# Seventy-eight TensorE matmuls into an unread PSUM bank behind the last output transposes of a streaming encoder layer

## The chip, the cores and the metric

The kernel runs on one core of a Trainium2 chip. The metric is the device time of one execution in microseconds (us), the median over a few executions. The profile is that of one execution, taken by the hardware profiler.

## The reference

One layer of a hybrid encoder is computed for 1024 prompt frames (one new stream) and 32 sample frames (a running stream with caches):

```python
h = rms_norm(x, g_mix);  z = h @ w_in
rq, rk, rv, rg, dq, dk, dv, ga, gb = split(z)
branch_a = (rms_norm(retention(rope(rq), rope(rk), rv)) * silu(rg)) @ w_ret_br
branch_b = (rms_norm(diff_attention(dq, dk, dv), g_dnorm) * (1 - lam_init)) @ w_da_br
x = x + (sigmoid(ga) * branch_a + sigmoid(gb) * branch_b) @ w_out
u = rms_norm(x, g_ffn) @ w_up
x = x + (silu(cg) * cv) @ w_down            # cg, cv: causal depthwise conv of u
x = x + sigmoid(rms_norm(x, g_ple) @ w_ple_gate) * (ple @ w_ple)
```

It returns y for both streams, the new keys and values, the retention states and the last rows for the convolution. The width is 1024, the hidden width 2816, all data are float32.

## The kernel before

Activations lie feature-major in SBUF: 128 features on the partitions, 1056 token columns (1024 prompt and 32 sample) in the free dimension, cut into three thirds of 352 (`THIRD`). Every large product is made of three matmuls on reduced float32 (`F32R`) operands, high by high, high by low and low by high (`three`, lines 639 to 641); `w_hi` and `w_lo` are the two parts of the weights in eight slots, `a_hi` and `a_lo` those of the activations. GpSimd splits the weights, SyncE loads them, ScalarE and VectorE empty PSUM. All work is placed by hand: each engine has one written-out program, and semaphores order them.

The change stands at the end of TensorE's program. There the last stage runs over eight feature tiles m: the gate product (`gate_product`, 72 matmuls of 352 columns), then the small product of the per-layer input (`ple_product`, 18 of them), and `out_rows(m - 1)` (line 1129) in between: nine transposes against `ident`, line 1141, that turn 128 features back into token rows, into PSUM banks 6 and 7 and, for the 32 sample rows, another bank. For m = 7 the transposes wait for VectorE third by third (`y_done`, lines 1138 to 1140). ScalarE copies banks 6 and 7 out (line 1755) and sends the rows to `y_prompt` (line 1759); VectorE copies the 32 sample rows (line 2332) and SyncE sends them (line 525).

Then the block closes (line 109): each engine drains its queue and adds to a semaphore, GpSimd waits until all have, and releases them all. ScalarE comes to its own drain only when the last stores have landed, since its program ends with waits on `y_st` and `ul_st` (lines 1769 to 1771).

Tile m = 7 uses weight slot 5 (`PG_SLOTS[7 % 3]`) for its gate; that slot, `a_hi` and `a_lo` are not written again. Banks 0 to 2 hold the last accumulators, 0, 6 and 7 the last output rows; bank 4 was last read for m = 6.

Of the kernel before, what the change touches and what calls it, by code (L numbers as in the profile page):

```python
# [22 lines left out]
P = 128  # L23
# [84 lines left out]
def kernel_program(nc, t):  # L108
    with ExitStack() as ctx:
        def sb(name, shape, dt=F32):  # L110
            return ctx.enter_context(nc.sbuf_tensor(name, shape, dt))
# [8 lines left out]
        w_hi = sb("w_hi", [P, SLOTS, 8 * P], F32R)  # L120
        w_lo_at = -(-nc.sbuf_base // 32) * 32
        w_lo = sb("w_lo", [P, SLOTS, 8 * P], F32R)

        x_late = nc.alloc_sbuf_tensor_at("x_late", [P, 4, D], F32, offset=w_lo_at + 4 * 4 * 8 * P)
        a_hi = sb("a_hi", [P, KT * NT], F32R)
        a_lo_at = -(-nc.sbuf_base // 32) * 32
        a_lo = sb("a_lo", [P, KT * NT], F32R)
# [16 lines left out]
        ps = ctx.enter_context(nc.psum_tensor("ps", [P, 8, 512], F32))  # L144
# [141 lines left out]
        at = nrm_at + 256  # L286
# [349 lines left out]
        def _(pe):  # L636
# [492 lines left out]
            def out_rows(m):  # L1129

                for part, (i0, i1) in enumerate(((0, 4), (4, 8), (8, 9))):
                    if part < 2 and m:
                        pe.wait_ge(S["y_ev"], 3 * m - 2 + part)
                    for i in range(i0, i1):
                        r = rows(i)
                        if m < 7:
                            if i == 0:
                                pe.wait_ge(S["y_done"], m + 1)
                        elif i in (0, 2, 5):
                            pe.wait_ge(S["y_done"], m + 1 + (0, 2, 5).index(i))  # L1140
                        last = pe.transpose(ps[0:r, row_bank(m, part), (i % 4) * P:(i % 4 + 1) * P],
                                            x(m)[:, i * P:i * P + r], ident[:, :])
                    last.then_inc(S["y_tr"], 1)
# [98 lines left out]
            last_ple_product()  # L1242
            out_rows(7)


        @block.scalar
        def _(act):
# [1136 lines left out]
```

## Time and profile before

| | |
|---|---|
| device time, median of 3 runs | 2210.62 us (2210.6 to 2211.06) |
| span of the profiled execution, first to last instruction | 2209.2 us |
| median less that span | 1.4 us |
| TensorE (PE) busy in the span | 2201.9 us, 13110 matmuls |
| weight loads (PEld) | 2088.3 us, 13110 |
| VectorE (DVE), ScalarE (ACT), GpSimd (POOL) | 1089.5, 704.5, 666.3 us |

The span is the time of the profiled execution itself, from its first to its last instruction; the 1.4 us to the median lie around it. A matmul's row lasts longer than the spacing of the starts, since matmuls are pipelined: the cost of one in a row of them is read from the distance between starts. Registers, branches, semaphores and DMA issues don't count as busy; they carry a q behind the engine's name (PEldq is TensorE's queue).

### The profile page before, as it was taken

How to read it: one execution, taken by the hardware profiler on the slowest of the kernel's cores; microseconds unless marked ns; L12 is line 12 of the kernel's file. 1: busy time of each engine (PE TensorE's matmuls, PEld its weight loads, DVE VectorE, ACT ScalarE, POOL GpSimd, SP SyncE). 2: the span in 40 equal slices, each digit the busy share in tenths (PEclk: the TensorE clock that was granted, in tenths of full speed). 3: DMA queues.
4: the chain of work that ended last, by engine and by line, in shares of the span. 5: the costliest groups of instructions: out<-in, count | busy, mean ns of one | idle time of the engine just before them, and what ended most of it. 6: DMA issues, size and time to landing. Idle time of an engine off the chain costs nothing.

```text
span 2209.2 us, 34227 instructions
## 1 busy us (share of the span) xinstructions
PE 2201.9 (100%) x13110; PEld 2088.3 (95%) x13110; DVE 1089.5 (49%) x2076; ACT 704.5 (32%) x1654; POOL 666.3 (30%) x368
## 2 busy tenths in 40 slices
PE   9999999999999999999999999999999999999999
PEld 9999777789898898998999999999999999999999
DVE  6212444555646456364155568676666663313432
ACT  5201333335555555555221131101111113434311
POOL 5422220230310401303152353233332226576420
PEclk9999999999999999999999999999999999999999
DMA  8622222230220301304652322222122226656311
GB/s 266 205 83 73 72 81 82 73 107 25 64 83 30 115 29 31 114 27 159 228 181 62 107 80 68 68 68 77 60 75 67 72 73 201 182 167 202 94 49 50
DMA packets 312670, 218.19 MB, mean 99 GB/s; under 512 B 16332, under 2 KB 303679, under 8 KB 312544
## 3 DMA queue, kind: packets, MB, share of 16 engines
q1 hardware_dynamic: 219802, 117.33, 18.4%
q10 hardware_dynamic: 92742, 99.15, 13.4%
q8 instruction: 83, 1.36, 0.3%
q14 instruction: 43, 0.35, 0.1%
HBM read 160.15 MB, written 56.29 MB: 98 GB/s over the span
## 4 chain that ended last, share of the span: by engine, by line
PE 99%; DVE 0%; DMA 0%; issue 0%; ACT 0%; ACTq 0%; DVEq 0%
PE ps L639 28%; PE ps L641 28%; PE ps L640 28%; PE ps L931 3%; PE ps L904 3%; PE ps L779 1%; PE ps L780 1%; PE ps L922 1%; PE ps L850 1%; PE ps L855 1%; PE ps L1066 1%; PE ps L852 1%; PE ps L907 0%; PE ps L868 0%; PE ps L1082 0%; PE ps L834 0%
## 5 line engine op out<-in xcount | busy, mean ns | idle before, releaser
L639 PE MATMUL ps<-a_hi,w_hi 128*128 128x352 f32 x2920 | 946.8, 324 | 0.0
L641 PE MATMUL ps<-a_hi,w_lo 128*128 128x352 f32 x2920 | 936.9, 321 | 0.0
L640 PE MATMUL ps<-a_lo,w_hi 128*128 128x352 f32 x2920 | 936.3, 321 | 0.0
L537 POOL TENSOR_SCALAR w_hi<-w_raw 128x1024 fp32r<-128x1024 f32 x150 | 162.9, 1086 | 1404.4 <-PE ps L641 659.9
L639 PEld LDWEIGHTS ps<-a_hi,w_hi 128*128 128x128 f32 x2920 | 547.8, 188 | 3.4 <-issue 2.7
L640 PEld LDWEIGHTS ps<-a_lo,w_hi 128*128 128x128 f32 x2920 | 548.9, 188 | 0.4
L641 PEld LDWEIGHTS ps<-a_hi,w_lo 128*128 128x128 f32 x2920 | 548.4, 188 | 0.0
L539 POOL TENSOR_TENSOR w_lo<-w_raw,w_hi 128x1024 fp32r<-128x1024 f32 x150 | 363.8, 2425 | 12.5
L639 PE MATMUL ps<-w_hi,a_hi 128*128 128x384 f32 (+1 forms) x768 | 283.3, 369 | 0.0
L641 PE MATMUL ps<-w_hi,a_lo 128*128 128x384 f32 (+1 forms) x768 | 273.3, 356 | 0.0
L640 PE MATMUL ps<-w_lo,a_hi 128*128 128x384 f32 (+1 forms) x768 | 273.0, 355 | 0.0
L614 POOL TENSOR_TENSOR w_lo<-w_raw,w_hi 128x1024 fp32r<-128x1024 f32 (+1 forms) x64 | 141.4, 2240 | 74.2 <-ACT w_hi L1687 74.2
L641 PEld LDWEIGHTS ps<-w_hi,a_lo 128*128 128x128 f32 x768 | 144.2, 188 | 11.4
L640 PEld LDWEIGHTS ps<-w_lo,a_hi 128*128 128x128 f32 x768 | 144.9, 189 | 9.9
L639 PEld LDWEIGHTS ps<-w_hi,a_hi 128*128 128x128 f32 x768 | 144.5, 188 | 10.1
L1640 ACT ACT_TABLE_LOAD x21 | 26.9, 1283 | 253.0 <-issue 253.0
L2203 DVE TENSOR_TENSOR scr<-ps,scr 128x704 f32<-128x704 f32 x44 | 39.2, 891 | 132.0 <-PE ps L641 132.0
L2211 DVE COPY u_last<-scr 128x4 f32 (+1 forms) x44 | 88.3, 2006 | 5.7
L2249 DVE TENSOR_TENSOR full<-full,ps 128x352 f32 (+1 forms) x24 | 12.4, 520 | 155.9 <-PE ps L641 155.9
L1884 DVE TENSOR_TENSOR scr<-ps,full 128x128 f32<-128x128 f32 (+3 forms) x72 | 25.7, 356 | 117.0 <-ACT full L1354 115.8
L1354 ACT ACTIVATE full<-ps,u_last 128x256 f32<-128x256 f32 (+1 forms) x36 | 17.0, 472 | 204.3 <-PE ps L641 192.9
L1640 ACT ACTIVATE scr<-scr 128x1058 f32<-128x1058 f32 x22 | 24.0, 1090 | 182.2 <-DVE scr L2219 182.2
(230 smaller groups left out, 2522.5 us busy)
## 6 DMA issues: line engine op xcount, KB each, us to landing
w_raw<-w_in SPq DMA_DIRECT2D x64, 512.0 KB, 4.3
w_raw<-w_down SPq DMA_DIRECT2D x48, 512.0 KB, 3.7
w_raw<-w_up SPq DMA_DIRECT2D x44, 512.0 KB, 3.8
hid_d<-scr ACTq DMA_DIRECT2D x22, 512.0 KB, 2.6
w_raw<-w_down SPq DMA_DIRECT2D x24, 384.0 KB, 3.3
scr<-gates_d ACTq DMA_DIRECT2D x24, 352.0 KB, 6.2
gates_d<-full ACTq DMA_DIRECT2D x13, 528.0 KB, 2.6
xt_d<-full ACTq DMA_DIRECT2D x1, 4224.0 KB
```

The lines of the kernel that those rows point to most:

```text
L537: pool.tensor_scalar(hi, raw, 1.0, 0.0, ALU.mult, ALU.add).then_inc(S["w_hi_done"], 1)
L539: pool.tensor_tensor(lo, raw, hi.bitcast(F32), ALU.subtract).then_inc(S["w_split"], 1)
L614: pool.tensor_tensor(w_lo[:, slot, 0:words], w_raw[:, j % RAW, 0:words], w_hi[:, slot, 0:words].bitcast(F32), ALU.subtract).then_inc(S["w_ ...
L639: pe.matmul(out, lhs[0], rhs[0], start=start, stop=False)
L640: pe.matmul(out, lhs[0], rhs[1], start=False, stop=False)
L641: return pe.matmul(out, lhs[1], rhs[0], start=False, stop=stop)
L904: last = pe.matmul(ps[0:r, score_bank(m, i) + b // 512, 0:n], q_t[:, i % 2, m, 0:r], k_t[:, m, first + b:first + b + n], start=True, stop= ...
L931: last = pe.matmul(ps[0:r, 7, 0:DV], a_t[0:n, b, 0:r], v_tok[0:n, vt, :], start=b == 0, stop=b == every - 1)
L1640: act.activation(row(1, CW), row(1, CW), ACT.Silu).then_inc(S["silu_done"], 1)
L1884: dve.tensor_tensor(bb[:, :, 0, :], x4[:, :, 1, :], sn, ALU.mult).then_inc(prods, 1)
L2203: dve.tensor_tensor(u[:, GAP:GAP + 2 * THIRD].rearrange("p (c n) -> p c n", c=2), src[:, 0:2, :], inv[:, 0:2 * THIRD].rearrange("p (c n) - ...
L2211: dve.tensor_copy(u_last[:, bass.ds(j + half * FT, 1), :].rearrange("p a (s w) -> p (a s) w", w=GAP), ends).then_inc(S["u_last_done"], 1)
```

## The change

Behind `out_rows(7)`, the last work of TensorE's program, 78 matmuls are added. They wait for no semaphore and add to none. All write bank 4, and nothing reads that bank afterwards.

```diff
             last_ple_product()
             out_rows(7)
+
+            def resident(n, at=0, m=P, stationary=w_hi[:, 5, 0:P], moving=a_hi, bank=4, times=6):
+
+                for _ in range(times):
+                    pe.matmul(ps[0:m, bank, 0:n], stationary[:, 0:m], moving[:, at:at + n], start=True, stop=True)
+
+            resident(512)
+            resident(352)
+            resident(264)
+            resident(352, at=32)
+            resident(352, at=8)
+            resident(264, at=264)
+            resident(352, stationary=a_hi[:, 4096:4096 + P], moving=w_hi[:, 5, :])
+            resident(256)
+            resident(352, m=64)
+            for _ in range(4):
+                for lhs, rhs, bank in ((w_hi, a_hi, 4), (w_hi, a_lo, 4), (w_lo, a_hi, 4)):
+                    pe.matmul(ps[:, bank, 0:264], lhs[:, 5, 0:P], rhs[:, 0:264], start=True, stop=True)
+            resident(128)
+            resident(32)
```

The loops are Python's: the program holds 78 separate matmuls, each with its weight load. By moving width they are 6 of 512 columns, 30 of 352 (five calls: two with a shifted start, one with the operands' parts exchanged, one with 64 stationary columns), 24 of 264, 6 of 256, 6 of 128 and 6 of 32. No other engine's program is touched.

## Rows read from the trace of the kernel before

**Rows 1.** The page: the span and the engines' busy time
```profile
span 2209.2 us, 34227 instructions
PE 2201.9 (100%) x13110; PEld 2088.3 (95%) x13110; DVE 1089.5 (49%) x2076; ACT 704.5 (32%) x1654; POOL 666.3 (30%) x368
PE 99%; DVE 0%; DMA 0%; issue 0%; ACT 0%; ACTq 0%; DVEq 0%
q8 instruction: 83, 1.36, 0.3%
```
**Rows 2.** The timeline of the last 3 us: start, duration, engine, line, shapes
```profile
2205.24 0.66 PE L1141 MATMUL ps<-ident,full 128*128 128x128 f32 x4 [0.44 <-DVE full L2329]
2205.82 0.59 ACT L1755 COPY scr<-ps 128x512 f32<-128x512 f32 x1 [0.46 <-PE ps L1141]
2206.44 0.38 ACTq L1759 DMA_DIRECT2D y_prompt<-scr  x1
```
**Rows 3.** Line 109, the block's close: operation, count, duration in ns, start in us
```profile
L109 PEldq DRAIN  x1: 700/700/700, 2205.2 to 2205.2; - x1
L109 ACTq DRAIN  x1: 8/8/8, 2209.0 to 2209.0; - x1
L109 PEldq EVENT_SEMAPHORE  x1: 51/51/51, 2209.2 to 2209.2; - x1
```
**Rows 4.** Stretches at the end: busy time by engine, granted clock, DMA share, GB/s
```profile
2200.00:2205.00 5.00, 4.69 (x33) 4.18 (x31) 3.30 (x7) 2.40 (x5) 0.00 (x0) 1.00 0.22 65
2205.00:2209.20 4.20, 0.66 (x4) 0.38 (x4) 0.46 (x2) 0.95 (x2) 0.00 (x0) 1.00 0.64 180
2205.00:2210.00 5.00, 0.66 (x4) 0.38 (x4) 0.46 (x2) 0.95 (x2) 0.00 (x0) 0.93 0.54 151
```
**Rows 5.** Timeline of TensorE in the last gate product, 352 columns
```profile
2197.51 0.32 PE L639 MATMUL ps<-a_hi,w_hi 128*128 128x352 f32 x1
2197.66 0.32 PE L640 MATMUL ps<-a_lo,w_hi 128*128 128x352 f32 x1
2197.82 0.32 PE L641 MATMUL ps<-a_hi,w_lo 128*128 128x352 f32 x1
...
2198.47 0.32 PE L639 MATMUL ps<-a_hi,w_hi 128*128 128x352 f32 x1
```
**Rows 6.** Timeline of TensorE, 512 columns, 128 stationary columns
```profile
256.93 0.39 PE L641 MATMUL ps<-w_hi,a_lo 128*128 128x512 f32 x1
...
258.30 0.40 PE L641 MATMUL ps<-w_hi,a_lo 128*128 128x512 f32 x1
```
**Rows 7.** The same with 64 stationary columns
```profile
248.51 0.39 PE L779 MATMUL ps<-w_hi,pair 128*64 128x512 f32 x1
...
249.88 0.39 PE L779 MATMUL ps<-w_hi,pair 128*64 128x512 f32 x1
```
**Rows 8.** Timeline of TensorE, narrow matmuls in a row
```profile
1.07 3.58 PE L710 MATMUL ps<-ones 128*128 128x128 f32 x16 [1.07 <-DVE ones L1776]
5.87 1.06 PE L710 MATMUL ps<-ones 128*128 128x128 f32 x8
27.62 0.68 PE L683 MATMUL ps<-ident,x_late 32*128 32x32 f32 x8
```
**Rows 9.** Groups by shape: line, engine, shapes, count, busy us, mean ns
```profile
L710 PE MATMUL ps<-ones 128*128 128x128 f32 x46 | 7.3, 324 | 1.1 <-DVE ones L1776 1.1
L683 PE MATMUL ps<-ident,x_late 32*128 32x32 f32 x8 | 0.7, 224 | 0.0
L639 PEld LDWEIGHTS ps<-a_hi,w_hi 128*128 128x128 f32 x2920 | 547.8, 188 | 3.4 <-issue 2.7
L779 PEld LDWEIGHTS ps<-w_hi,pair 128*64 128x64 f32 x96 | 12.9, 135 | 4.7
```
**Rows 10.** The chain of waits, float32 of 256 columns: start, length in us, engine, line, count
```profile
883.07 1.73 PE ps L931 x8
```

## The prediction

> **What bounds the kernel now.** I read the page first. TensorE is busy in 2201.9 of 2209.2 us, and 99% of the chain that ended last is TensorE's [rows 1]. So whatever is added to TensorE ahead of its last output would cost its full length. The change stands behind that output, where the share says nothing: there the question is what ends last in the final 4 us.
>
> For that I read the timeline of the tail. TensorE's last four transposes start at 2205.24 us and their row ends at 2205.90; ScalarE copies them out from 2205.82 and issues the last store at 2206.44 [rows 2]. Then no engine computes. The reader is to see in the stretches that between 2205.0 and 2209.2 TensorE is busy for 0.66 us and the DMA engines for 64% [rows 4]: the tail is the landing of the last store. The rows of line 109 show how it ends: TensorE's queue is drained at 2205.2 + 0.70 = 2205.9, ScalarE's only at 2209.0, and the release reaches TensorE at 2209.2 [rows 3]. TensorE therefore lies idle for 3.1 us behind its last transpose, and any work that is shorter than this would be free there. From the last engine's drain to the end of the span it takes 0.2 us.
>
> **What the change adds.** Nothing is removed or moved, no wait and no semaphore is added, and no DMA. 78 matmuls, each with a weight load, stand behind the last transpose in TensorE's queue. What is queued behind them is TensorE's drain, and GpSimd waits for that drain before it releases the engines. The outputs are not behind them: ScalarE, VectorE and SyncE wait for the transposes' semaphores, which are given before.
>
> The cost is the spacing of starts, not the length of a row, since two rows overlap. At 352 columns six starts take 2198.47 - 2197.51 = 0.96 us, so 0.160 us for one [rows 5]. At 512 columns it is (258.30 - 256.93) / 6 = 0.228 us [rows 6]. That is 0.455 and 0.446 ns a column: the cost goes by the columns, with hardly a fixed part. For 264 and 256 columns, which the trace doesn't show with reduced operands, I take 0.455 ns a column from the nearer width: 0.120 and 0.116 us. With 64 stationary columns the spacing is (249.88 - 248.51) / 6 = 0.228 us at 512 columns [rows 7], the same as with 128, so the call with m=64 is priced as the others. The exchanged operands and the shifted starts I price like the plain ones: the kernel already runs either order (activations stationary in rows 6, weights in rows 5) at nearly the same price a column. The shifts themselves have no row; they can't be cheaper than a plain one, and I hold their risk with the upper end below.
>
> The narrow ones, 128 and 32 columns, have no row with reduced operands either. Nearest are the float32 ones: eight of 128 columns take 1.06 us, or (1.06 - 0.27) / 7 = 0.11 us each if the last lasts some 0.27 us (an estimate from the eight rows' own end), and eight of 32 columns, each lasting 0.224 us, take 0.68 us, or 0.065 us [rows 8, 9]. A weight load bounds them too: 64 more stationary columns lengthen it by 188 - 135 = 53 ns [rows 9], so 128 take an estimated 0.11 us of the loading path. All twelve load 128 columns, so I take 0.11 us for each.
>
> The sum at full clock:
> - 6 of 512: 6 x 0.228 = 1.37 us
> - 30 of 352: 30 x 0.160 = 4.80 us
> - 24 of 264: 24 x 0.120 = 2.88 us
> - 6 of 256: 6 x 0.116 = 0.70 us
> - 12 narrow: 12 x 0.11 = 1.32 us
>
> Together 11.07 us. TensorE's drain moves from 2205.9 to 2216.97, behind ScalarE's at 2209.0; it now ends last, and with 0.2 us for the release the span is 2217.2 us, 8.0 more. Of the 11.07 us 3.1 are hidden by the last store's landing; if that cover were gone the whole would be paid. The profiled span stands 1.4 us below the median and I keep this difference: 2210.62 + 8.0 = **2218.6 us**.
>
> **Bounds.** Below: at the full level of 2.4 GHz, which the granted 1.00 is [rows 4], one column a cycle is 0.417 ns. The 21504 columns of the wide ones then take 8.96 us, and the narrow ones by their columns alone 0.4 us: 9.36 us, a span of 2215.5, a time of 2216.9; with some 0.4 us for the end of the last matmul against the drain, which the rows give to a tenth only, 2216.4. Above: all widths that the trace lacks cost what float32 costs. Eight rows of 256 float32 columns take 1.73 us, 0.216 us each or 0.84 ns a column [rows 10]; 24 x 0.223 + 6 x 0.216 = 6.65 us in place of 3.58, and narrow ones at two rows each (46 rows come from 23 float32 matmuls of that line [rows 9]) 12 x 0.23 = 2.76 in place of 1.32. The sum is 15.6 us, the time 2223.1. I stay with the price a column, since the two reduced widths shown agree on it within 2%. The code of the added part has to be loaded too; over the whole span 83 loads left TensorE's weight loads 2.7 us of idle issue time [rows 1, 9], and one such load more is a fraction of that.
>
> The Trainium skill (TensorE: Matmul & The Clock Gate, Back-to-back issue gap) gives a warm spacing of N / 2.4 + 2.5 ns; here the trace has 160 ns for 352 columns, where that rule has 149. By it the 78 would take some 9.6 us, and the time would be 2217.1 us; the row decides.
>
> **The rivals.**
> 1. *Deeper overlap.* Each row of 352 columns lasts 0.32 us and starts come 0.16 apart [rows 5], so two are in flight. Six matmuls in a row with the same stationary operand might keep three in flight: 0.107 us for 352 columns, 0.303 ns a column, 6.5 us for the wide ones and 0.8 for narrow ones at 0.065: 7.3 us in all, and the time 2214.8, just inside 0.2%. Against it: 0.303 ns is under one column a cycle at the highest level, and the kernel's own chains show nothing below 0.44. The same section of the Trainium skill states a sustained spacing of about 131 ns at 512 columns, below the single gap; by it the time would be some 2213.8 us, and this trace has 228 ns for that width. Chance 3%.
> 2. *Not in the time: not slower.* The bank isn't read, so the added work may be dropped, or the close may not wait for it. The place is the drain of line 109, and the price is zero. It decides at 3.1 us: whatever part of the added work the close waits for beyond that is paid. The time would be 2210.6 us. Against it: TensorE's drain lasted 0.70 us, just until its last transposes' row ended [rows 2, 3], and it takes part in the release like ScalarE's. Chance 4%.
> 3. *Half clock.* If TensorE's clock fell to the half level (1.2 GHz), say since the transposes with their waits keep it only partly busy from 2203.6 to 2205.9, the added part would run slower. The kernel's first 16 narrow matmuls start (3.58 - 0.32) / 15 = 0.217 us apart, eight later ones 0.113 [rows 8, 9]; the ratio 1.92 is the nearest row that I have to a slow clock, though the record grants none there. 11.07 x 1.92 = 21.3 us, and the time is 2228.8. Against it: the granted clock is 1.00 up to the end of the span, 3.3 us after TensorE's last row, and falls only past it, as the share of 0.93 of the stretch up to 2210 tells [rows 4]. The longest gap ahead of the added part is 0.44 us [rows 2]. Chance 5%.
> 4. *Unshown shapes at the float32 price*, the upper bound above: 2223.1 us. For it speaks only that no row excludes it. Chance 8%.
>
> **How the numbers follow.** The forecast has 80%, the rivals 3, 4, 5 and 8%. The range goes from the lower bound, 2216.4, to the unshown shapes at 2223.2, and holds 88%. A measurement of this kernel tells apart some 0.2%, or 4.4 us. The forecast, rivals 3 and 4 are slower by more: 93%. Rivals 1 and 2 lie within: 6% with the part of rival 1 that goes over left out, and 1% for faster, for which I know no mechanism.
>
> **What would show it.** Right: 78 more matmuls and 78 more weight loads; a span near 2217.2 us; a chain whose last 8 us are TensorE's new lines; TensorE's drain after 2216, some 8 us behind ScalarE's, which stays at 2209.0; spacings of 0.23, 0.16, 0.12, 0.12 us by width, the same for shifted, exchanged and 64-column calls; granted clock 1.00 up to the end; everything before 2205.9 unmoved. Wrong: a spacing at 264 or 256 columns off the line, narrow matmuls with two rows each, a drop of the clock inside the added part, a call with a shifted start slower than the plain one, or ScalarE's drain still last.

## The result

| | before | changed |
|---|---|---|
| device time, median of 5 runs | 2210.62 us (2210.49 to 2211.06) | 2219.15 us (2218.77 to 2219.37) |
| ratio | | 1.0037, 95% interval 1.0023 to 1.0051 |
| span of the profiled execution | 2209.2 us | 2217.0 us |
| TensorE | 13110 matmuls | 13188 matmuls, 2213.6 us busy |

The kernel is 8.5 us, or 0.4%, slower; the forecast was 8.0 us. The interval goes from 5.1 to 11.3 us: the timing shows that the kernel is slower, and the rows of the traces show by how much. The page of the changed kernel counts 78 more matmuls and 78 more weight loads and as many instructions as before on VectorE, ScalarE and GpSimd; TensorE has 99% of the chain as before, against [rows 1]:

```profile
span 2217.0 us, 34383 instructions
PE 2213.6 (100%) x13188; PEld 2099.7 (95%) x13188; DVE 1090.4 (49%) x2076; ACT 704.8 (32%) x1654; POOL 666.9 (30%) x368
PE 99%; DVE 0%; DMA 0%; issue 0%; ACT 0%; ACTq 0%; DVEq 0%
```

A share of 99% says nothing of the last microseconds, here as in the kernel before. The end of the chain of waits says it, first in the kernel before, then in the changed one (start, length in us, engine, line, count; line 1248 is the matmul of `resident`, 1261 that of the alternating triples, 1141 the transposes, 1755 ScalarE's copy):

```profile
2205.24 0.56 PE ps L1141 x3
2205.82 0.59 ACT scr L1755
```

```profile
2205.07 0.66 PE ps L1141 x4
2205.73 8.37 PE ps L1248 x54
2214.10 1.44 PE ps L1261 x12
2215.54 1.25 PE ps L1248 x12
```

The chain used to leave TensorE at the last transposes and go to ScalarE's copy; now it stays on TensorE for another 11.06 us. The rows of line 109 (operation, count, duration in ns, start in us), against [rows 3]:

```profile
L109 ACTq DRAIN  x1: 8/8/8, 2208.8 to 2208.8; - x1
L109 PEldq DRAIN  x1: 2125/2125/2125, 2214.7 to 2214.7; - x1
L109 PEldq EVENT_SEMAPHORE  x1: 51/51/51, 2217.0 to 2217.0; - x1
```

ScalarE, whose outputs have landed, is done at 2208.8; TensorE's drain ends at 2214.7 + 2.1 = 2216.8, eight microseconds later, and the release follows after the same 0.2 us. The timeline of TensorE's tail shows what fills them (start, duration, engine, line, shapes; neighbours of one line and name are merged under the first one's shape):

```profile
2205.07 0.66 PE L1141 MATMUL ps<-ident,full 128*128 128x128 f32 x4 [0.45 <-DVE full L2349]
2205.49 5.98 PE L1248 MATMUL ps<-a_hi,w_hi 128*128 128x512 f32 x36
2211.31 1.13 PE L1248 MATMUL ps<-w_hi,a_hi 128*128 128x352 f32 x6
2212.27 1.82 PE L1248 MATMUL ps<-a_hi,w_hi 128*128 128x256 f32 x12
2213.93 0.28 PE L1261 MATMUL ps<-a_hi,w_hi 128*128 128x264 f32 x1
...
2215.38 1.41 PE L1248 MATMUL ps<-a_hi,w_hi 128*128 128x128 f32 x12
```

From start to start of the groups: the exchanged operands take 2212.27 - 2211.31 = 0.96 us for six, 0.160 us each; six of 256 columns and six of 352 with 64 stationary columns 1.66 us together, where 0.116 and 0.160 give 1.66 (apart they take 0.120 and 0.157, since the first with 64 starts at 2212.99); twelve alternating ones of 264 columns 1.45 us, 0.121 each; the twelve narrow ones 1.41 us with the last one's length in it. The merged row of 36 hides the shifted starts. In very short stretches a row begins with a single matmul. These six begin with the first and the fourth plain one of 352 columns, the first plain one of 264, the first and the eleventh shifted one of 352, and the first shifted one of 264:

```profile
2206.96 0.48 PE L1248 MATMUL ps<-a_hi,w_hi 128*128 128x352 f32 x2
2207.44 0.48 PE L1248 MATMUL ps<-a_hi,w_hi 128*128 128x352 f32 x2
2207.93 0.53 PE L1248 MATMUL ps<-a_hi,w_hi 128*128 128x264 f32 x3
2208.65 0.49 PE L1248 MATMUL ps<-a_hi,w_hi 128*128 128x352 f32 x2
2210.26 0.48 PE L1248 MATMUL ps<-a_hi,w_hi 128*128 128x352 f32 x2
2210.58 0.52 PE L1248 MATMUL ps<-a_hi,w_hi 128*128 128x264 f32 x3
```

Plain, 352 columns: (2207.44 - 2206.96) / 3 = 0.160 us. Shifted by 32 and by 8: (2210.26 - 2208.65) / 10 = 0.161. 264 columns: (2208.65 - 2207.93) / 6 = 0.120; shifted by 264: (2211.31 - 2210.58) / 6 = 0.122. A shifted start and exchanged operands make no difference that these rows could tell. The stretches (length, then busy time and count of TensorE, weight loads, VectorE, ScalarE, GpSimd, then granted clock, DMA share, GB/s), against [rows 4]:

```profile
2205.00:2210.00 5.00, 4.92 (x31) 4.65 (x32) 0.30 (x2) 0.79 (x2) 0.00 (x0) 1.00 0.52 142
2210.00:2215.00 5.00, 5.00 (x38) 4.88 (x37) 0.00 (x0) 0.00 (x0) 0.00 (x0) 1.00 0.00 0
2215.00:2217.02 2.02, 1.78 (x17) 1.68 (x15) 0.00 (x0) 0.00 (x0) 0.00 (x0) 1.00 0.00 0
```

Behind 2210 nothing but TensorE works, at the full clock.

### The profile page after: what moved, and what is told of

It is laid out like the page before. It is cut to its first block, busy times and chain, and to the rows that moved or that the text cites. A ratio compares the mean times of both kernels' runs of the same rounds, so it can differ in the third digit from the quotient of the medians.

```text
span 2217.0 us, 34383 instructions
## 1 busy us (share of the span) xinstructions
PE 2213.6 (100%) x13188; PEld 2099.7 (95%) x13188; DVE 1090.4 (49%) x2076; ACT 704.8 (32%) x1654; POOL 666.9 (30%) x368
## 4 chain that ended last, share of the span: by engine, by line
PE 99%; DVE 0%; DMA 0%; issue 0%; ACT 0%; ACTq 0%; DVEq 0%
PE ps L639 28%; PE ps L641 28%; PE ps L640 28%; PE ps L931 3%; PE ps L904 3%; PE ps L779 1%; PE ps L780 1%; PE ps L922 1%; PE ps L850 1%; PE ps L855 1%; PE ps L1066 1%; PE ps L852 1%; PE ps L907 0%; PE ps L1248 0%; PE ps L868 0%; PE ps L1082 0%
```

## The experiments

The theory: what stands behind the last output is paid from the moment at which TensorE's drain passes ScalarE's, and costs the spacing of its starts. The rivals are that the whole part is paid or that its price is fixed, that the place doesn't matter, that narrow matmuls cost by columns or by a fixed floor rather than by their weight load, and that the clock could have made it dearer. Times are medians, and each experiment's ratio is to the kernel before on the same chip in the same session (its medians there were 2211.12 us for the two narrow ones and for float32, and 2211.25 for the other four). The edits are shown against the changed kernel; `...` stands for lines left out.

**A part shorter than the cover.**

```diff
-            resident(512)
-            ...
-            resident(32)
+            resident(352, times=18)
```

> In place of the 78, 18 matmuls of 352 columns stand behind the last transposes. Theory A (the added part is paid only as far as TensorE's drain comes after ScalarE's at 2209.0): 18 x 0.160 = 2.9 us end at 2205.9 + 2.9 = 2208.8, just ahead of 2209.0, so the span stays 2209.2 and the time is within 0.5 us of the kernel before, 2210.6. Rival B (everything behind the last transposes is paid in full, since the tail scales with TensorE's queue): 2210.6 + 2.9 = 2213.5 us. Beside it: the changed kernel's time stood 1.8 us above its span and the one before's 1.4; if this 0.4 us belongs to more code in TensorE's program, it is about a quarter here (0.1), if it belongs to TensorE's being the last to drain, it is absent here.

Measured: 2211.23 us, ratio 0.9998 (0.9989 to 1.0008). Line 109:

```profile
L109 PEldq DRAIN  x1: 3045/3045/3045, 2206.1 to 2206.1; - x1
L109 ACTq DRAIN  x1: 8/8/8, 2209.3 to 2209.3; - x1
```

TensorE is done at 2206.1 + 3.05 = 2209.15, just ahead of ScalarE at 2209.3: eighteen matmuls of 352 columns cost nothing. Rival B, 2.9 us or a ratio of 1.0013, is out. The interval of about 0.1% (2 us) leaves room for a fraction of the 2.9 us, so the drain rows carry the point together with the ratio.

**The part twice.**

```diff
             resident(32)
+            resident(512)
+            ...
+            resident(32)
```

> The 78 matmuls stand twice, 156 in all. Theory A (each further matmul costs its spacing, the cover is spent once): 11.07 us more than the changed kernel, 2219.15 + 11.1 = 2230.2 us, with the second block's spacings equal to the first's. Rival B (the cover grows with the part, or the measured 8.5 us are a fixed price of having TensorE drain last): 2219 to 2228 us. Rival C (the clock falls in the longer stretch): above 2232 us with a granted clock below 1.00 ahead of the end. If the 0.4 us outside the span come from the amount of code, the time stands some 2.2 us above the span here; if from TensorE draining last, 1.8 again.

Measured: 2230.44 us, ratio 1.0086 (1.0069 to 1.0103). Line 1248 (form, count, duration in ns, first and last start) in the changed kernel and here, and then two stretches, one in each block:

```profile
L1248 PE MATMUL ps<-a_hi,w_hi x60: 220/303/481, 2205.5 to 2216.5; 128*128 128x352 f32 x18, 128*128 128x264 f32 x12, 128*128 128x512 f32 x6, 128*128 128x256 f32 x6
L1248 PE MATMUL ps<-a_hi,w_hi x120: 220/302/481, 2206.1 to 2228.2; 128*128 128x352 f32 x36, 128*128 128x264 f32 x24, 128*128 128x512 f32 x12, 128*128 128x256 f32 x12
```

```profile
2210.00:2216.00 6.00, 6.00 (x46) 5.88 (x45) 0.00 (x0) 0.00 (x0) 0.00 (x0) 1.00 0.00 0
2222.00:2228.00 6.00, 6.00 (x48) 5.88 (x48) 0.00 (x0) 0.00 (x0) 0.00 (x0) 1.00 0.00 0
```

From the first start to the last it takes 2228.2 - 2206.1 = 22.1 us where one block in the changed kernel takes 2216.5 - 2205.5 = 11.0. The second block costs all of its spacings, 11.3 us by the medians and 10.8 by the ratios: the cover is spent once and the price is not fixed. The ratio's interval alone would leave room for the upper end of rival B; the spacings exclude it. The clock stayed full, so rival C is out too.

**The part ahead of the last transposes.**

```diff
+            resident(512)
+            ...
+            resident(32)
             out_rows(7)
-            resident(512)
-            ...
-            resident(32)
```

> The same 78 stand ahead of the last nine transposes in place of behind them. Theory A: the landing of the last store no longer hides any of it. The nine transposes wait for nothing any more and take some 1.0 us in place of 2.1, so they end about 10.0 us later than before, and ScalarE's second copy, now behind its first copy and that one's store (0.59 + 0.6 us), starts some 10.8 us later, at 2216.6; the span ends 3.4 us behind it, at 2220.0, the time 2221.4 to 2221.9 us, 2 to 3 us above the changed kernel. Rival B (the place makes no difference, the work is paid the same on either side of the transposes): 2219.2 us.

Measured: 2222.39 us, ratio 1.0050 (1.0033 to 1.0067). The tail of its timeline:

```profile
2215.07 1.20 PE L1141 MATMUL ps<-ident,full 128*128 128x128 f32 x9
2215.81 0.58 ACT L1774 COPY scr<-ps 128x512 f32<-128x512 f32 x1 [12.66 <-PE ps L1141]
2216.85 0.58 ACT L1774 COPY scr<-ps 128x512 f32<-128x512 f32 x1 [0.46 <-ACT scr L1774]
```

And line 109:

```profile
L109 PEldq DRAIN  x1: 2200/2200/2200, 2214.1 to 2214.1; - x1
L109 ACTq DRAIN  x1: 8/8/8, 2220.1 to 2220.1; - x1
```

The nine transposes wait for nothing and take 1.20 us in one row, the second copy waits for ScalarE itself and not for TensorE, and the span ends at 2220.4, 3.5 us behind the start of that copy. TensorE is drained at 2216.3, ScalarE at 2220.1, so the landing of the last store ends the kernel again. The same work is dearer ahead of the output than behind it, by 2.9 us going by the ratios (1.0050 and 1.0037) and 3.4 by the spans (2220.4 and 2217.0). The intervals of the two ratios overlap; it is the rows that put rival B out: the place gives the cover. The time lies 0.5 us above the top of what I expected; the profiled span is 0.4 us longer, since the nine transposes took 1.20 us and the second copy started at 2216.85.

**78 narrow matmuls, 128 stationary columns.**

```diff
-            resident(512)
-            ...
-            resident(32)
+            resident(32, times=78)
```

> In place of the 78 of mixed widths, 78 matmuls of 32 columns, each with 128 stationary columns. Theory A (a narrow one costs its weight load, 0.11 us, whatever its columns): 78 x 0.111 = 8.7 us, TensorE's drain at 2214.6, span 2214.8, time 2216.4 us. Rival B (columns alone, 0.455 ns each: 15 ns): 1.1 us, hidden, time 2210.6. Rival C (a fixed floor of some 0.06 us for each matmul as the 32-column transposes showed): 5.1 us, span 2211.2, time 2212.8.

Measured: 2220.71 us, ratio 1.0043 (1.0027 to 1.0060), 4 us above every expectation. Three rows of the timeline, all 78 and then two short stretches, the group of line 1248 (loads and matmuls, shortest, median and longest in ns), and three stretches with the clock:

```profile
2205.75 13.41 PE L1248 MATMUL ps<-a_hi,w_hi 128*128 128x32 f32 x78
2205.97 0.49 PE L1248 MATMUL ps<-a_hi,w_hi 128*128 128x32 f32 x3
2218.14 0.59 PE L1248 MATMUL ps<-a_hi,w_hi 128*128 128x32 f32 x2
```

```profile
L1248 PEld LDWEIGHTS ps<-a_hi,w_hi x78: 190/333/338, 2205.7 to 2218.7; 128*128 128x128 f32 x78
L1248 PE MATMUL ps<-a_hi,w_hi x78: 262/374/376, 2205.7 to 2218.8; 128*128 128x32 f32 x78
```

```profile
2205.75:2209.40 3.65, 3.65 (x36) 3.65 (x33) 0.28 (x1) 0.59 (x1) 0.00 (x0) 1.00 0.56 157
2209.60:2213.00 3.40, 3.40 (x17) 3.40 (x18) 0.00 (x0) 0.00 (x0) 0.00 (x0) 0.50 0.00 0
2213.00:2219.40 6.40, 6.15 (x29) 6.04 (x29) 0.00 (x0) 0.00 (x0) 0.00 (x0) 0.50 0.00 0
```

At first the spacing is the 0.11 us of theory A: (0.49 - 0.26) / 2, with 0.26 us for the last one's length. Between 2209.4 and 2209.6 the granted clock falls to 0.50, that is from 2.4 to 1.2 GHz, and the spacing becomes 0.59 - 0.37 = 0.22 us. Had it stayed at 0.11, the 78 would have taken 8.7 us; at 13.41 they take 4.7 more, which is the miss. The price of a narrow matmul is settled by the first 3.7 us alone; what I had not expected is the clock. TensorE counts as busy from the first of the 78 to the last, so the share of busy time did not announce it. All four timed runs of this kernel had the same mean clock, 0.998, where those of the changed kernel had 1.0. Why the clock fell here is not shown.

**The same with 32 stationary columns.**

```diff
-            resident(32, times=78)
+            resident(32, m=32, times=78)
```

> The same 78 of 32 columns, but with 32 stationary columns in place of 128. Theory A (the weight load is the bound): a load of 64 columns was 53 ns shorter than one of 128, so 32 columns take about a quarter of 0.11 us, and the spacing falls to whatever floor stands below it, at most the 0.065 us of the narrow transposes: at most 5.1 us in all, time at most 2212.8 us, and if the floor is below 0.039 us all of it is hidden and the time is 2210.6. Rival B (a fixed price of 0.11 us for each narrow matmul, whatever its weights): the same as with 128 stationary columns, 2216.4 us.

Measured: 2211.02 us, ratio 1.0000 (0.9990 to 1.0009). One row of the timeline, the group of line 1248, and line 109:

```profile
2205.44 2.70 PE L1248 MATMUL ps<-a_hi,w_hi 128*32 128x32 f32 x78
```

```profile
L1248 PEld LDWEIGHTS ps<-a_hi,w_hi x78: 110/113/113, 2205.4 to 2207.9; 128*32 128x32 f32 x78
L1248 PE MATMUL ps<-a_hi,w_hi x78: 182/183/260, 2205.4 to 2208.0; 128*32 128x32 f32 x78
```

```profile
L109 PEldq DRAIN  x1: 720/720/720, 2207.4 to 2207.4; - x1
L109 ACTq DRAIN  x1: 8/8/8, 2208.8 to 2208.8; - x1
```

All 78 fit in 2.70 us and are hidden: TensorE is drained at 2208.1, ScalarE at 2208.8. With the same 32 columns moving, a quarter of the stationary columns takes about a quarter of the time. The spacing is (2.70 - 0.18) / 77 = 0.033 us, 0.18 us being the last one's length, against 0.11 with 128 columns at full clock. So the stationary columns set the price of a narrow matmul, and rival B is out. That it is the load itself is argued from the load rows: at full clock they last 0.190 us with 128 columns and 0.113 with 32, 0.077 us less, as much as the spacing falls. But `m` narrows the output together with the load, and no run here separates the two.

The Trainium skill (TensorE: Matmul & The Clock Gate, LDWEIGHTS (loading the stationary operand)) gives columns / 1.2 ns for a load, by which I estimate 107 and 27 ns here. The spacings agree with it at 128 columns (0.11 us) and lie 6 ns above it at 32.

**An idle gap ahead of the part.**

```diff
+            pe.wait_ge(S["ul_st"], 80)
             resident(512)
...
             act.wait_ge(S["ul_st"], 64)
+            act.dma_start(inv_d, row(0)[0:1, 0:NT]).then_inc(S["ul_st"], 16)
```

> The 78 stand where the change has them, but TensorE first waits for a small further store (4 KB) that ScalarE issues once all outputs have landed, so that it lies idle from 2205.9 to about 2211. Three outcomes. Clock kept: 2211 + 11.1 + 0.2 = 2222.3 span, time 2223.9. Clock at half through the first 3.6 us, as in the first 16 narrow matmuls of the kernel before (3.58 us), and full afterwards: about 1.8 us more, 2225.7. Clock at half throughout: 2211 + 21.3, time 2234. Theory: the record of before shows the clock falling between 2209.2 and 2210, so I expect the middle one, and the record to grant 0.5 at the start of the part. It tells what the prediction's third rival would have cost, and that the change escapes it since TensorE has no such gap.

Measured: 2226.21 us (2225.03 to 2227.57), ratio 1.0069 (1.0052 to 1.0085). Four stretches:

```profile
2205.80:2207.50 1.70, 0.00 (x0) 0.00 (x0) 0.28 (x1) 0.51 (x1) 0.00 (x0) 0.81 0.71 196
2207.50:2209.90 2.40, 0.00 (x0) 0.00 (x0) 0.00 (x0) 0.00 (x0) 0.00 (x0) 0.50 0.30 88
2210.00:2213.70 3.70, 3.70 (x10) 3.12 (x11) 0.00 (x0) 0.00 (x0) 0.00 (x0) 0.50 0.00 0
2213.80:2218.00 4.20, 4.20 (x31) 4.20 (x30) 0.00 (x0) 0.00 (x0) 0.00 (x0) 1.00 0.00 0
```

The middle outcome: the part starts at the half level and goes at full clock from about 2213.7. In 3.7 us at half it got through ten matmuls (six of 512 columns and four of 352, about 2.0 us at the full-clock spacings), and that cost about 1.8 us. The profiled run, at 2225.03 us the fastest of the four, started the part at 2209.99 and not at the 2211 that I had expected; from there 11.1 + 0.2 + 1.8 us, and 1.8 us more from span to time, give 2224.9. So the stretches carry the verdict, and the nearness of the median to the expected 2225.7 does not. But the fall came earlier than I had thought possible: the first stretch, from the end of the last transposes, has a mean of 0.81, so 0.38 of its 1.70 us, or 0.65 us, lie at the half level, and the clock fell near 2206.85, some 1.1 us after the last transpose. In the kernel before it held for over 3.3 us [rows 4]. TensorE's program is the same up to that point; why the clock fell at different times is not shown.

**Plain float32 in place of the reduced type, twelve matmuls of 264 columns.**

```diff
-                    pe.matmul(ps[:, bank, 0:264], lhs[:, 5, 0:P], rhs[:, 0:264], start=True, stop=True)
+                    pe.matmul(ps[:, bank, 0:264], lhs[:, 5, 0:P].bitcast(F32), rhs[:, 0:264].bitcast(F32), start=True, stop=True)
```

> The changed kernel, but twelve of its 264-column matmuls read the same bytes as plain float32. Theory A (a float32 matmul is two rows at 0.84 ns a column each, as line 931 shows: 0.445 us for 264 columns): 12 x (0.445 - 0.120) = 3.9 us more, time 2223.1 us, and twelve more matmul rows. Rival B (one row each at 0.223 us, the price of the prediction's upper bound): 1.2 us more, 2220.4 us. Rival C (no difference between the two types at this width): 2219.2 us.

Measured: 2222.74 us, ratio 1.0053 (1.0037 to 1.0070). The timeline of the triples:

```profile
2213.84 0.61 PE L1261 MATMUL ps<-a_hi,w_hi 128*128 128x264 f32 x2
2214.29 0.61 PE L1261 MATMUL ps<-a_lo,w_hi 128*128 128x264 f32 x2
2214.73 0.61 PE L1261 MATMUL ps<-a_hi,w_lo 128*128 128x264 f32 x2
```

Each of the twelve is two rows now, and they start (2214.73 - 2213.84) / 2 = 0.445 us apart in place of 0.120. That is 3.9 us for twelve; the spans differ by 2220.8 - 2217.0 = 3.8 us, the medians by 3.6. The ratio's interval alone would leave room for rival B; the rows exclude it, and theory A holds.

## Why the prediction was right, and where it was off

- *What bounds the end.* Right. The 3.1 us between TensorE's drain and ScalarE's were cover, the rest was paid: the short part cost nothing, the doubled one cost the whole second block, and ahead of the output the cover was lost.
- *The sum.* Right to 0.1 us, in part by terms that cancel. It had 11.07 us from the end of the last transposes' row to TensorE's drain; after, the transposes' row ends at 2205.73 and the drain at 2216.8. Single terms: 264 columns at 0.120 us as taken from the price a column at 352, shifts and exchange at the plain price, narrow ones 0.11 us at full clock. The six of 256 columns came out a little dearer (0.120 for 0.116) and those with 64 stationary columns a little cheaper (0.157 for 0.160), with the forecast's sum of 1.66 us. The six of 512 columns took 2206.96 - 2205.49 = 1.47 us where the sum has 1.37: the first, behind the transposes, 0.32 us and the other five 0.23 each. Against that the first one starts 0.24 us before the transposes' row ends, which the sum doesn't count; nor does it count the length of the last row beyond its spacing.
- *The difference to the median.* This is the term that was off, and it makes most of the 0.5 us between 2218.6 and 2219.15: the median run has a span of 2217.4, 0.2 us above the forecast's, and stands 1.75 us above it in place of 1.4. I kept 1.4 us from the median before less the profiled span. But nothing ties the two to one execution. In the five runs after, the time stands 1.75 to 1.87 us above the same run's span, and so it does in runs of the kernel before beside the experiments (2210.24 us over a span of 2208.5, 2211.12 over 2209.3). That points to an execution of about 2211.0 us behind the profile before, near the top of the runs shown; 2217.2 + 1.8 gives 2219.0. The short part (2211.38 over 2209.6) and the doubled one (2230.52 over 2228.7) have 1.8 us too, so neither the amount of code nor TensorE's draining last, which the expectations weighed, is needed. That the forecast came within 0.5 us is also luck: beside the experiments, runs of the kernel before went from 2209.64 to 2213.10 us.
- *The load of code.* The 78 pairs brought no stall: TensorE's spacings go on without a gap through all of the added part, and the page's line for the instruction queue has the same 83 packets as before [rows 1]. The 2.7 us that I set beside those 83 are the idle time of a single group of loads [rows 9], not of all of TensorE's, so they were no measure of the price.
- *Deeper overlap* didn't come: six equal matmuls in a row keep 0.160 us like the kernel's own chains. Six of 512 columns, the first behind the transposes included, took 0.245 us each on average. The Trainium skill (TensorE: Matmul & The Clock Gate, Back-to-back issue gap) states a sustained 131 ns or so for that width, and these rows, at 245, don't agree. The Trainium skill's other rule in that section, N / 2.4 + 2.5 ns, gives an estimated 112 ns for 264 columns; the rows have 120.
- *Not in the time* is out by the drain rows: the close waits for matmuls whose bank nobody reads.
- *Half clock* didn't come, and the stretches grant 1.00 to the end, as do all five timed runs. But one reason that I gave against it was weak. I read from the kernel before that the clock holds 3.3 us after the last row; with the idle gap it fell after 1.1 us. In the change the part follows the transposes at once and is mostly wide, and the granted clock stayed at 1.00; with an idle gap ahead it began at 0.50, and with narrow matmuls of 128 stationary columns alone it fell to 0.50 on the way. The price for a stretch was about right: a ratio of 1.92 was taken, and the narrow ones went from 0.11 to 0.22 us. The row that it came from doesn't show a slow clock, though: the record grants 1.00 at those first 16 matmuls, and what slowed them stays open.
- *Unshown shapes at the float32 price* didn't come. The bound itself was too low for its name: a float32 matmul of 264 columns costs 0.445 us in two rows, and I had counted one row of 0.223 for the 264 and 256 columns. With 0.445 and 0.432 the sum would have been 15.6 + 24 x 0.222 + 6 x 0.216 = 22.2 us, and the time 2229.7.

## What to carry to other kernels

In this kernel, work behind the last output was free up to the landing of the last store (3.1 us) and paid in full beyond it. Find the end of such a cover in the drains at the program's close, not in the share of busy time. Price a chain of matmuls by the spacing of starts: here it went by the moving columns for wide ones (0.160 us at 352) and by the stationary columns for narrow ones (0.11 us at 128, 0.033 at 32). Take the time around the span from the same execution as the span. Where matmuls are added to keep TensorE's clock, look at the granted clock itself: in the run of 78 narrow ones it fell while every row counted as busy.

## What the runs showed of the hardware that I had not expected

- A chain of 78 matmuls of 32 moving and 128 stationary columns keeps TensorE busy in every stretch of the record, and the granted clock still fell to 0.50 some 3.7 us into it and did not come back in the 9.8 us up to the end of the span. The changed kernel's 78 of mixed widths, and the 22 us of them in the doubled part, kept 1.00.
- After the same transposes the clock fell some 1.1 us into an idle gap in one execution and had not fallen 3.3 us into it in another.
- Matmuls of 32 moving columns with 32 stationary columns start every 0.033 us; with 128 stationary columns, at full clock, every 0.11 us.
- Matmuls into a bank that nobody reads still hold up the program's close: TensorE's drain ended at 2216.8, ScalarE's at 2208.8, and the span at 2217.0.
